# Rotary halves of the queries and keys exchanged by ScalarE copies instead of a product with a constant matrix

## The chip, the cores and the metric

The kernel runs on one core of a Trainium2 chip. The metric is the time of one execution on the device in microseconds (us), as the median over the runs of a kernel. All data are 32-bit floats.

The engines are called as the profile calls them: PE (TensorE, matrix products), PEld (its weight loads), DVE (VectorE), ACT (ScalarE), POOL (GpSimd) and SP (SyncE, which here only issues the weight DMAs). SBUF is the on-chip memory of 128 partitions, PSUM the eight accumulation banks that PE writes.

## The reference, cut to what matters

Two layers of attention plus a mixture of experts on 512 tokens of width 1024, followed by a second block. Only the start of each of the two layers is touched: the query, key and value projections and the rotary embedding of queries and keys.

```python
def rope(t, cos, sin):
    half = t.shape[-1] // 2
    t1, t2 = t[..., :half], t[..., half:]
    return jnp.concatenate([t1 * cos - t2 * sin, t2 * cos + t1 * sin], axis=-1)

for l in range(DEPTH):                       # DEPTH = 2
    proj = x @ w_in[l]                       # (512, 1024) @ (1024, ...)
    q, k, v, cb, cc, cu, qm, gates = jnp.split(proj, IN_SPLITS, axis=-1)
    q = rope(q.reshape(B, S, 16, 64), cos, sin)
    k = rope(k.reshape(B, S, 16, 64), cos, sin)
    ...                                      # attention, convolution, memory attention, merge, experts
```

A head vector has 64 entries; the first 32 and the last 32 are its two halves. Each half is multiplied by the cosine, and the other half, multiplied by the sine (with a minus sign for the first half), is added.

## The kernel before

**Stage.** `qkv` (L736 to L805) is one stage per layer. It makes six chunks n = 0 to 5, each the product of the tokens (`XT`, features in partitions) with a 1024 x 512 slice of `w_in`. Chunks 0 and 1 are the queries, 2 and 3 the keys, 4 and 5 the values. For queries and keys a chunk leaves four tiles c = 0 to 3 of 128 x 512 in `raw` (buffers `B[3]`, `B[4]`), features in partitions, two head vectors of 64 in each tile. The rotated result goes to `out` (`B[0]`, `B[1]`).

**Seven products.** `SevenProducts` (L541 to L723) computes a chunk as a 2 x 2 block product with seven block products instead of eight. The weight sums that this needs are made by POOL (`sum_weights`, L579 to L589: four adds of 128 x 1024 for each chunk, SBUF to SBUF). The token sums are made once in a stage by DVE (L572 to L577). PE runs the seven parts of a chunk (`multiply`, L591 to L664) in the order first, fifth, sixth, third, seventh, second, fourth for n > 0; each part is two halves i = 0, 1 of four 128x256 products, all issued from L600. ACT copies parts out of PSUM as they come (`keep_first`, `keep_fifth`, `keep_sixth`, `last_quarter`; all recorded as L728). DVE adds the rest (`add_sums`: `upper_right` L693, `corner` L699, `upper_left` L705). PE waits for some of it inside the chunk: sixth half i waits for `keep_first` half i (L636), third for `keep_fifth` (L616), seventh for `keep_sixth` (L643), and fourth half i waits for `corner` half i (L622), because it accumulates into the bank that `corner` has read.

**Rotary.** In chunks n = 1 to 4, PE pauses after the first part (`pause`, L650) and runs `rotate(n - 1)` (L759 to L766): for each of the four tiles of the chunk before, one 128x128 by 128x512 product with the constant `rotate`, a signed permutation matrix, into bank 6 or 7. DVE does `turn(n - 1)` (L785 to L797) before the `add_sums` of chunk n: four products tile x cosine (L789), then for each tile bank x sine (L793) and the sum (L796). Each product of `rotate` for c = 2, 3 waits until DVE has read the bank of c - 2 (L764).

**Order.** Every engine runs its own instruction list in the order written; they meet by semaphores. A stage ends in a barrier of all engines. The weight chunks come through a ring of four 2 MB slots; SP issues the load of chunk n + 2 (and its sums get their slot) when the fourth part of chunk n is done (`last_use`, L664). POOL's sums for chunk n + 1 start when that load has landed, which is during chunk n.

**Sine table.** `angle_tables` makes `sin` and `cos` (128 x 512 each) once at the start, `sin` by one ACT instruction (L480). The constants, `rotate` among them, are loaded by one DMA; PE waits for it just before its first `rotate` (L761).

Of the kernel before, what the change touches and what calls it, by code (L numbers as in the profile page):

```python
# [23 lines left out]
ALU = mybir.AluOpType  # L24
ACT = mybir.ActivationFunctionType
AX = mybir.AxisListType.X

P = 128
# [22 lines left out]
TWO_PI_1, TWO_PI_2, TWO_PI_3 = 6.28125, 0.0019340515136718750, 1.2556659146e-06  # L51


CONST_NAMES = ["ident", "ones", "ones_over_d", "head_ones", "rotate", "causal", "earlier",
               "chunk_lower", "chunk_upper", "chunk_upper_incl"]


def constants():
    i = np.arange(P)
    chunk = i // 32  # L60
    same = chunk[:, None] == chunk[None, :]
    rot = np.zeros((P, P), np.float32)
    for m in range(P):
        if m % 64 < 32:
            rot[m + 32, m] = -1.0
        else:
            rot[m - 32, m] = 1.0
    tables = {
        "ident": np.eye(P),
        "ones": np.ones((P, P)),  # L70
        "ones_over_d": np.full((P, P), 1.0 / D),
        "head_ones": (i[:, None] // 64 == i[None, :] // 64),
        "rotate": rot,
        "causal": np.where(i[None, :] <= i[:, None], 0.0, -1e30),
        "earlier": (i[:, None] < i[None, :]),
        "chunk_lower": same & (i[:, None] > i[None, :]),
        "chunk_upper": same & (i[:, None] < i[None, :]),
        "chunk_upper_incl": same & (i[:, None] <= i[None, :]),
    }
    c = np.stack([tables[n] for n in CONST_NAMES], 1).astype(np.float32)  # L80
    t = np.arange(SEQ)
    rows = np.stack([np.broadcast_to(t % 32 != 0, (P, SEQ)), np.broadcast_to(t, (P, SEQ))], 1)
    inv_freq = (10000.0 ** (-np.arange(0, 64, 2) / 64)).astype(np.float32)
    small = np.zeros((P, 64), np.float32)
    small[:, 0] = inv_freq[i % 32]
    small[:, 1:17] = 16 - np.arange(16)
    small[:, 17:21] = 4 - np.arange(4)
    small[:, 24:24 + N_OVER] = np.arange(N_OVER) * P
    small[:, 48:64] = np.arange(E_N) * P
    return c, rows.astype(np.float32), small  # L90


INV_FREQ, EXPERT_KEY, GROUP_KEY = slice(0, 1), slice(1, 17), slice(17, 21)
OVER_START, HOME_SLOT = slice(24, 24 + N_OVER), slice(48, 64)


# [213 lines left out]
class Machine:  # L310
    def __init__(self, nc, ctx, dram):
        self.nc, self.ctx, self.dram = nc, ctx, dram
        sb, sem = self.sb, self.sem
        self.const = sb("const", [P, len(CONST_NAMES), P])
        self.small = sb("small", [P, 64])
# [32 lines left out]
    def sb(self, name, shape, dt=F32):  # L348
        return self.ctx.enter_context(self.nc.sbuf_tensor(name, shape, dt))
# [4 lines left out]
    def c(self, name):  # L354
        return self.const[:, CONST_NAMES.index(name), :]

# [29 lines left out]
    def issue_weights(self, block):  # L386

        @block.sync
        def _(sp):
            static = {n: i for i, n in enumerate(static_names())}  # L390
            while self.issued < len(self.stream):
# [3 lines left out]
                if i == 1:  # L395
                    sp.wait_ge(self.ring_full[0], 16)
                    sp.wait_ge(self.x_loaded, 16)
                    for dst, src in ((self.const[:, :, :], self.dram["consts"]), (self.par[:, :], self.dram["params"]),
                                     (self.rt[:, 3 * P:4 * P], self.dram["consts"][:, CONST_NAMES.index("causal"), :])):
                        sp.dma_start(dst, src).then_inc(self.loaded, 16)  # L400
# [58 lines left out]
def angle_tables(m):  # L459

    ang, k, half = m.T[0], m.T[1], m.T[2]
    with m.stage() as block:
        @block.vector
        def _(dve):
            pos = m.B[4][:, 0, :].bitcast(I32)
            dve.tensor_copy(ang[:, :], pos).then_inc(m.tally("dve_step").up(), 1)
            dve.wait_ge(*m.tally("dve_step").last())
            dve.tensor_scalar(ang[:, :], ang[:, :], m.small[:, INV_FREQ], None, ALU.mult).then_inc(m.tally("dve_step").up(), 1)
            dve.wait_ge(*m.tally("dve_step").last())
            reduce_angle(m, dve, ang, k)  # L470

    with m.stage() as block:
        @block.sync
        def _(sp):
            for dst, src in ((m.memT[:, :, :], m.dram["memT"]), (m.wr[:, :, :], m.dram["w_router"])):
                sp.dma_start(dst, src).then_inc(m.memory_loaded, 16)

        @block.scalar
        def _(act):
            act.activation(m.sin[:, :], ang[:, :], ACT.Sin)  # L480
            act.activation(half[:, :], ang[:, :], ACT.Sin, scale=0.5).then_inc(m.tally("half_sine").up(), 1)

        @block.vector
        def _(dve):
            dve.wait_ge(*m.tally("half_sine").at(1))
            dve.tensor_tensor(half[:, :], half[:, :], half[:, :], ALU.mult).then_inc(m.tally("dve_step").up(), 1)
            dve.wait_ge(*m.tally("dve_step").last())
            dve.tensor_scalar(m.cos[:, :], half[:, :], -2.0, 1.0, ALU.mult, ALU.add)
# [43 lines left out]
def blocks(*tiles):  # L532

    out = []
    for t in tiles:
        v = t.rearrange("p (q a) (b t) -> p q (a b) t", a=2, b=2)
        out += [v[:, i] for i in range(2)]
    return out
# [187 lines left out]
def copy_to(dest):  # L726

    return lambda act, p, h, i, src: act.activation(dest(p, h, i), src, ACT.Copy)  # L728


def within(tile):

    return lambda p, h, i: tile(2 * p + i)[:, HALF * h:HALF * h + HALF]


def qkv(m, l):  # L736

    bk = m.banks
    raw = [m.B[3], m.B[4]]
    out = [m.B[0], m.B[1]]  # L740
    seven = SevenProducts(m, m.XT, blocks(m.B[5][:, 0:4, :], m.B[5][:, 4:8, :]))

    def dest(n):
        if n < 4:
            return within(lambda c: raw[n // 2][:, 4 * (n % 2) + c, :])
        return lambda p, h, i: m.B[2][:, 2 * (2 * h + i) + n - 4, HALF * p:HALF * p + HALF]

    with m.stage() as block:
        for n in range(6):
            seven.chunk(("in", l, n))  # L750
            if 0 < n < 5:
                for c in range(4):
                    bk.plan(("rot", l, n - 1, c), 6 + c % 2)

        @block.tensor
        def _(pe):
            pe.wait_ge(m.x_loaded, 16)

            def rotate(n):  # L759
                if (l, n) == (0, 0):  # L760
                    pe.wait_ge(m.loaded, m.load_n)  # L761
                for c in range(4):
                    seven.finished(pe, n, c // 2, c % 2)
                    pe.wait_ge(*bk.vacant(("rot", l, n, c)))  # L764
                    bank = bk.bank(("rot", l, n, c))
                    pe.matmul(bank[:, :], m.c("rotate"), raw[n // 2][:, 4 * (n % 2) + c, :], start=True, stop=True).then_inc(bk.full_sem(("rot", l, n, c)), 1)  # L766

            for n in range(6):
                seven.multiply(pe, n, tokens_left=n >= 4, pause=(lambda: rotate(n - 1)) if 0 < n < 5 else None)

        @block.scalar
        def _(act):
            for n in range(6):
                for part in (seven.keep_first, seven.keep_fifth, seven.keep_sixth, seven.last_quarter):
                    part(act, n, copy_to(dest(n)))

        @block.gpsimd
        def _(pool):
            for n in range(6):
                seven.sum_weights(pool, n)  # L780

        @block.vector
        def _(dve):

            def turn(n):  # L785
                tile = lambda c: (raw[n // 2][:, 4 * (n % 2) + c, :], out[n // 2][:, 4 * (n % 2) + c, :])
                for c in range(4):
                    seven.finished(dve, n, c // 2, c % 2)
                    dve.tensor_tensor(tile(c)[1], tile(c)[0], m.cos[:, :], ALU.mult).then_inc(m.tally("dve_step").up(), 1)  # L789
                for c in range(4):  # L790
                    dve.wait_ge(*bk.made(("rot", l, n, c)))
                    tmp = m.T[c % 2]
                    dve.tensor_tensor(tmp[:, :], bk.bank(("rot", l, n, c))[:, :], m.sin[:, :], ALU.mult).then_inc(bk.free_sem(("rot", l, n, c)), 1)  # L793
                    dve.wait_ge(*bk.read_done(("rot", l, n, c)))
                    dve.wait_ge(*m.tally("dve_step").last())
                    dve.tensor_tensor(tile(c)[1], tile(c)[1], tmp[:, :], ALU.add).then_inc(m.tally("dve_step").up(), 1)  # L796
                    dve.wait_ge(*m.tally("dve_step").last())  # L797

            dve.wait_ge(m.x_loaded, 16)
            seven.sum_tokens(dve)  # L800
            for n in range(6):
                if 0 < n < 5:
                    turn(n - 1)
                seven.add_sums(dve, n, dest(n))
        m.issue_weights(block)  # L805


# [2386 lines left out]
```

## Time and profile before

| | us |
|---|---|
| median of 3 runs (3727.48 to 3737.3) | 3736.56 |
| profiled execution, its own time | 3742.89 |
| span of that execution | 3741.2 |
| PE busy | 3309.7 (88%) |
| PEld busy | 2272.8 (61%) |
| DVE busy | 1497.7 (40%) |
| POOL busy | 769.6 (21%) |
| ACT busy | 715.3 (19%) |

The mean granted clock of TensorE over the span is 0.928 of full speed. In the profile a row `L600 PE MATMUL bank<-B,ring` is the group of PE products issued by line 600 that write a PSUM bank from buffer B and the weight ring; a bracket at the end of a row is the idle time of the engine before it and who ended it. A 32-bit product of one PE instruction in the code shows as two records. "2.99 PE x6" is six records merged over 2.99 us. The four busy shares of an average over the whole span say little about one stage, so the prediction reads the stage itself.

### The profile page before, as it was taken

The numbers are of one execution on the slowest core, as the hardware profiler recorded it, in microseconds if no ns is written. First come the engines' busy times: TensorE is split into PE (matmuls) and PEld (weight loads), VectorE is DVE, ScalarE is ACT, GpSimd is POOL, SyncE is SP. The second block draws the span as 40 slices with busy tenths as digits, with TensorE's granted clock in tenths as the row PEclk, the third lists the DMA queues.
The fourth block names the chain that finished last, engine by engine and source line by source line (L and its number), as shares of the span: only waits on it lengthen the run. The fifth ranks groups of instructions, "written<-read, shape, count | busy, mean of one in ns | idle before, by whom it ended". The sixth has DMA issues, their size and how long they took to land. (4 is left out here: it accounts for less than half of the span.)

```text
span 3741.2 us, 37361 instructions
## 1 busy us (share of the span) xinstructions
PE 3309.7 (88%) x14316; PEld 2272.8 (61%) x14316; DVE 1497.7 (40%) x2645; ACT 715.3 (19%) x1630; POOL 769.6 (21%) x490
## 2 busy tenths in 40 slices
PE   6989999959998598999998699947789899699996
PEld 5857767744444486776666344426567667488842
DVE  4364712331111545576644111134567522455502
ACT  1152211021111114323221111112222111111100
POOL 3314112300000340311002100003344322243200
PEclk9989999969999798999998899978889889899998
DMA  3141222227887111032232588832101122112210
GB/s 140 68 192 50 108 79 79 90 101 285 320 326 270 68 68 46 28 131 79 113 118 90 212 326 325 319 143 93 65 24 46 47 90 90 45 68 90 112 68 23
DMA packets 49365, 471.22 MB, mean 126 GB/s; under 512 B 5600, under 2 KB 5984, under 8 KB 25376
## 3 DMA queue, kind: packets, MB, share of 16 engines
q1 hardware_dynamic: 26784, 378.77, 27.6%
q0 software_dynamic: 20816, 76.03, 5.1%
q10 hardware_dynamic: 1584, 13.93, 0.9%
q8 instruction: 123, 2.02, 0.2%
q14 instruction: 58, 0.48, 0.0%
HBM read 507.76 MB, written 63.70 MB: 153 GB/s over the span
## 5 line engine op out<-in xcount | busy, mean ns | idle before, releaser
L600 PE MATMUL bank<-B,ring 128*128 128x256 f32 x4336 | 957.2, 381 | 38.1 <-PEq L1985 21.3
L600 PEld LDWEIGHTS bank<-B,ring 128*128 128x128 f32 x4336 | 828.5, 191 | 165.0 <-issue 49.4
L1788 PE MATMUL bank<-ring,B 128*128 128x512 f32 x1024 | 451.4, 599 | 1.8 <-issue 1.5
L584 POOL TENSOR_TENSOR ring<-ring 128x1024 f32<-128x1024 f32 x52 | 134.6, 2589 | 1258.7 <-DMA ring<-in_w_static 341.2
L728 ACT ACTIVATE B<-bank 128x256 f32<-128x256 f32 x356 | 135.8, 383 | 1117.6 <-PE bank L600 1093.9
L600 PE MATMUL bank<-XT,ring 128*128 128x256 f32 x1344 | 307.9, 383 | 45.0 <-PEq L812 28.9
L1788 PEld LDWEIGHTS bank<-ring,B 128*128 128x128 f32 x1024 | 193.7, 192 | 237.2 <-issue 235.0
L600 PEld LDWEIGHTS bank<-XT,ring 128*128 128x128 f32 x1344 | 258.2, 193 | 86.5 <-issue 51.3
L509 PE MATMUL bank<-B,ring 128*128 128x512 f32 x704 | 307.8, 596 | 2.0 <-issue 2.0
L509 PEld LDWEIGHTS bank<-B,ring 128*128 128x128 f32 x704 | 134.7, 191 | 164.6 <-issue 163.8
L1856 DVE TENSOR_TENSOR B<-B,bank 128x512 f32<-128x512 f32 x46 | 31.6, 687 | 492.7 <-PE bank L1788 480.7
L1807 PE MATMUL bank<-ring,B 128*128 128x512 f32 x512 | 226.3, 595 | 1.5 <-ACT B L1841 1.5
L1807 PEld LDWEIGHTS bank<-ring,B 128*128 128x128 f32 x512 | 95.0, 190 | 110.0 <-issue 110.0
L2976 PE MATMUL bank<-B,ring 128*128 128x512 f32 x352 | 153.8, 600 | 7.3 <-PEq L2888 7.3
L693 DVE TENSOR_TENSOR B<-bank,B 128x256 f32<-128x256 f32 x96 | 40.4, 424 | 280.7 <-PE bank L600 280.1
L588 POOL TENSOR_TENSOR ring<-ring 128x1024 f32<-128x1024 f32 x52 | 136.5, 2626 | 4.1
L586 POOL TENSOR_TENSOR ring<-ring 128x1024 f32<-128x1024 f32 x52 | 136.5, 2625 | 4.1
L1867 DVE COPY B<-bank 128x512 f32<-128x512 f32 x92 | 62.3, 690 | 184.6 <-PE bank L1807 182.0
L589 POOL TENSOR_TENSOR ring<-ring 128x1024 f32<-128x1024 f32 x52 | 134.1, 2578 | 0.0
L2976 PEld LDWEIGHTS bank<-B,ring 128*128 128x128 f32 x352 | 67.7, 193 | 93.0 <-issue 93.0
L699 DVE TENSOR_TENSOR B<-bank,B 128x256 f32<-128x256 f32 x98 | 41.6, 424 | 156.8 <-PE bank L600 156.8
L1832 ACT ACTIVATE B<-bank 128x512 f32<-128x512 f32 x92 | 50.3, 600 | 263.7 <-PE bank L1757 174.2
(439 smaller groups left out, 3928.2 us busy)
## 6 DMA issues: line engine op xcount, KB each, us to landing
ring<-in_w_expert SPq DMA_DIRECT2D x96, 2048.0 KB, 9.0
ring<-in_w_static SPq DMA_DIRECT2D x79, 2048.0 KB, 8.0
B<-in_w_expert SPq DMA_DIRECT2D x42, 2048.0 KB
slots_y<-B POOLq DMA_DIRECT2D x53, 512.0 KB, 27.1
B<-slots_x POOLq DMA_DIRECT2D x46, 512.0 KB
slots_x<-B POOLq DMA_DIRECT2D x23, 512.0 KB, 16.0
ring<-s_tables SPq DMA_DIRECT2D x4, 2048.0 KB, 7.8
s_tables<-tmp POOLq DMA_DIRECT2D x8, 512.0 KB, 3.8
```

The lines of the kernel that those rows point to most:

```text
L509: ins = pe.matmul(bank[:, :], w(k, col), rhs(k), start=k == 0, stop=k == kts - 1)
L584: pool.tensor_tensor(s(0), w(1, 0), w(1, 1), ALU.add).then_inc(made.up(), 1)
L586: pool.tensor_tensor(s(1), s(0), w(0, 0), ALU.subtract).then_inc(made.up(), 1)
L588: pool.tensor_tensor(s(3), w(0, 1), s(1), ALU.subtract).then_inc(made.up(), 1)
L589: pool.tensor_tensor(s(2), w(0, 0), w(1, 0), ALU.subtract).then_inc(made.up(), 1)
L600: ins = pe.matmul(out, left, right, start=start and k == 0, stop=k == 3, skip_group_check=not start)
L728: return lambda act, p, h, i, src: act.activation(dest(p, h, i), src, ACT.Copy)
L1788: ins = pe.matmul(bank[:, :], xbT[q % 2][:, k, :], slot[:, k, :], start=k == 0, stop=k == KT - 1)
L1807: ins = pe.matmul(bank[:, :], hidT[q % 2][:, k, :], slot[:, k, cols], start=k == 0, stop=k == 3)
L1832: act.activation(xbT[q % 2][:, 4 * i:4 * i + 4, :], bank[:, :].rearrange("p (a b) -> p a b", a=4), ACT.Copy).then_inc(bk.free_sem(("xbT", ...
L1867: dve.tensor_copy(y[o % 2][:, i, :], bank[:, :]).then_inc(bk.free_sem(("y", l, o, i)), 1)
L2976: ins = pe.matmul(bank[:, :], slot(k % 4, c), hidden_tile(m, k), start=k == 0, stop=k == FF_T - 1)
```

## The change

The constant `rotate` is dropped. `sin` gets its sign in the table: the ACT instruction that makes it takes a per-partition scale, -1 in the first 32 partitions of each 64 and +1 in the others (sin(-a) = -sin(a)). PE has no `rotate` and no pause. ACT copies the halves of each tile of `raw` crosswise into `out` (`exchange`: four copies of 32 partitions x 512 for each tile), one tile behind each of its existing parts of the chunk. DVE then multiplies `out` by the signed sine into a scratch tile, writes tile x cosine over `out`, and adds the scratch; it does tiles 0 and 1 before `add_sums` of the chunk and tiles 2 and 3 behind it. Banks 6 and 7 are no longer used in this stage.

```diff
-            act.activation(m.sin[:, :], ang[:, :], ACT.Sin)
+            act.activation(m.sin[:, :], ang[:, :], ACT.Sin, scale=m.small[:, HALF_SIGN])
...
@@ qkv, tensor engine
-            def rotate(n):
-                if (l, n) == (0, 0):
-                    pe.wait_ge(m.loaded, m.load_n)
-                for c in range(4):
-                    seven.finished(pe, n, c // 2, c % 2)
-                    pe.wait_ge(*bk.vacant(("rot", l, n, c)))
-                    bank = bk.bank(("rot", l, n, c))
-                    pe.matmul(bank[:, :], m.c("rotate"), raw[n // 2][:, 4 * (n % 2) + c, :], start=True, stop=True).then_inc(bk.full_sem(("rot", l, n, c)), 1)
             for n in range(6):
-                seven.multiply(pe, n, tokens_left=n >= 4, pause=(lambda: rotate(n - 1)) if 0 < n < 5 else None)
+                seven.multiply(pe, n, tokens_left=n >= 4)
+            if l == 0:
+                pe.wait_ge(m.loaded, m.load_n)
...
@@ qkv, scalar engine
+            def exchange(n, c):
+                seven.finished(act, n, c // 2, c % 2)
+                src, dst = raw[n // 2][:, 4 * (n % 2) + c, :], out[n // 2][:, 4 * (n % 2) + c, :]
+                for to, fro in ((0, 32), (32, 0), (64, 96), (96, 64)):
+                    ins = act.activation(dst[to:to + 32, :], src[fro:fro + 32, :], ACT.Copy)
+                ins.then_inc(m.tally("exchanged").up(), 1)
             for n in range(6):
-                for part in (seven.keep_first, seven.keep_fifth, seven.keep_sixth, seven.last_quarter):
+                for c, part in enumerate((seven.keep_first, seven.keep_fifth, seven.keep_sixth, seven.last_quarter)):
+                    if 0 < n < 5 and c == 3:
+                        exchange(n - 1, 3)
                     part(act, n, copy_to(dest(n)))
+                    if 0 < n < 5 and c < 3:
+                        exchange(n - 1, c)
...
@@ qkv, vector engine
-            def turn(n):
+            def turn(n, pair):
                 tile = lambda c: (raw[n // 2][:, 4 * (n % 2) + c, :], out[n // 2][:, 4 * (n % 2) + c, :])
-                for c in range(4):
-                    seven.finished(dve, n, c // 2, c % 2)
-                    dve.tensor_tensor(tile(c)[1], tile(c)[0], m.cos[:, :], ALU.mult)...
-                for c in range(4):
-                    ...
+                step = m.tally("dve_step")
+                for c in pair:
+                    dve.wait_ge(*m.tally("exchanged").at(4 * n + c + 1))
+                    dve.tensor_tensor(m.T[c % 2], tile(c)[1], m.sin[:, :], ALU.mult).then_inc(step.up(), 1)
+                dve.wait_ge(*step.last())
+                for c in pair:
+                    dve.tensor_tensor(tile(c)[1], tile(c)[0], m.cos[:, :], ALU.mult).then_inc(step.up(), 1)
+                dve.wait_ge(*step.last())
+                for c in pair:
+                    dve.tensor_tensor(tile(c)[1], tile(c)[1], m.T[c % 2], ALU.add).then_inc(step.up(), 1)
+                dve.wait_ge(*step.last())
...
                 if 0 < n < 5:
-                    turn(n - 1)
+                    turn(n - 1, (0, 1))
                 seven.add_sums(dve, n, dest(n))
+                if 0 < n < 5:
+                    turn(n - 1, (2, 3))
```

## Rows read from the trace of the kernel before

**Rows 1.** Stretches: length, busy us (instructions) by engine, granted clock, DMA share, GB/s.
```profile
55.72:84.17 28.45, 28.08 (x121) 22.64 (x120) 11.97 (x18) 3.07 (x8) 10.20 (x4) 1.00 0.20 75
169.54:194.00 24.46, 24.34 (x113) 21.09 (x111) 2.55 (x6) 3.16 (x9) 0.00 (x0) 1.00 0.23 86
1327.07:1355.52 28.45, 28.08 (x121) 22.63 (x120) 11.97 (x18) 3.07 (x8) 9.96 (x4) 1.00 0.20 74
```

**Rows 2.** Timeline of PE: start us, length us, records; first layer, then second.
```profile
55.72 3.62 PE L600 MATMUL bank<-XT,ring 128*128 128x256 f32 x16
59.17 2.99 PE L766 MATMUL bank<-B,const 128*128 128x512 f32 x6
62.52 1.10 PE L766 MATMUL bank<-B,const 128*128 128x512 f32 x2 [0.35 <-DVE tmp L793]
63.45 7.07 PE L600 MATMUL bank<-B,ring 128*128 128x256 f32 x32
...
148.82 7.07 PE L600 MATMUL bank<-ring,B 128*128 128x256 f32 x32
172.99 7.07 PE L600 MATMUL bank<-ring,B 128*128 128x256 f32 x32
...
1298.61 1.67 PE L600 MATMUL bank<-XT,ring 128*128 128x256 f32 x7
```

**Rows 3.** Instructions of line 766: durations in ns (minimum, median, maximum).
```profile
L766 PE MATMUL bank<-B,const x64: 592/592/668, 59.2 to 1391.3; 128*128 128x512 f32 x64
```

**Rows 4.** Timeline of ACT in chunk 1 of the first layer.
```profile
57.65 0.38 ACT L728 ACTIVATE B<-bank 128x256 f32<-128x256 f32 x1 [1.34 <-PE bank L600]
59.37 0.38 ACT L728 ACTIVATE B<-bank 128x256 f32<-128x256 f32 x1 [1.34 <-PE bank L600]
65.38 0.38 ACT L728 ACTIVATE B<-bank 128x256 f32<-128x256 f32 x1 [5.62 <-PE bank L600]
```

**Rows 5.** Groups of ACT instructions: busy us, mean ns; first a timeline row.
```profile
294.76 4.26 ACT L1074 ACTIVATE B<-B 128x512 f32<-128x512 f32 x8
...
L2468 ACT ACTIVATE B<-B 64x512 f32<-64x512 f32 x1 | 0.6, 630 | 0.0
L977 ACT ACT_TABLE_LOAD x3 | 3.8, 1283 | 3.5 <-PE bank L864 3.5
```

**Rows 6.** Timeline of POOL in the qkv stages.
```profile
35.59 3.21 POOL L588 TENSOR_TENSOR ring<-ring 128x1024 f32<-128x1024 f32 x1
63.91 2.85 POOL L584 TENSOR_TENSOR ring<-ring 128x1024 f32<-128x1024 f32 x1 [12.33 <-DMA ring<-in_w_static]
120.63 2.35 POOL L584 TENSOR_TENSOR ring<-ring 128x1024 f32<-128x1024 f32 x1 [17.92 <-DMA ring<-in_w_static]
123.06 2.68 POOL L586 TENSOR_TENSOR ring<-ring 128x1024 f32<-128x1024 f32 x1
125.82 2.68 POOL L588 TENSOR_TENSOR ring<-ring 128x1024 f32<-128x1024 f32 x1
128.46 2.35 POOL L589 TENSOR_TENSOR ring<-ring 128x1024 f32<-128x1024 f32 x1
1307.29 2.37 POOL L584 TENSOR_TENSOR ring<-ring 128x1024 f32<-128x1024 f32 x1 [12.40 <-DMA ring<-in_w_static]
```

**Rows 7.** Timeline of DVE in the qkv stage of the first layer.
```profile
30.05 3.25 DVE L574 TENSOR_TENSOR B<-XT,B 128x1024 f32<-128x1024 f32 x1
33.23 3.37 DVE L575 TENSOR_TENSOR B<-XT 128x1024 f32<-128x1024 f32 x1
61.69 0.69 DVE L793 TENSOR_TENSOR tmp<-bank,rotary 128x512 f32<-128x512 f32 x1
75.81 0.42 DVE L699 TENSOR_TENSOR B<-bank,B 128x256 f32<-128x256 f32 x1 [1.30 <-PE bank L600]
81.33 1.28 DVE L789 TENSOR_TENSOR B<-B,rotary 128x512 f32<-128x512 f32 x2
120.77 2.77 DVE L796 TENSOR_TENSOR B<-B,tmp 128x512 f32<-128x512 f32 x1
124.29 2.00 DVE L796 TENSOR_TENSOR B<-B,tmp 128x512 f32<-128x512 f32 x1
...
39.81 0.74 DVE L705 TENSOR_TENSOR B<-bank,B 128x256 f32<-128x256 f32 x2
```

**Rows 8.** Stretches of the attention stages of both layers, columns as in rows 1.
```profile
194.00:290.00 96.00, 78.42 (x368) 50.62 (x368) 68.29 (x256) 56.78 (x201) 16.99 (x31) 0.79 0.48 187
1437.00:1534.00 97.00, 79.65 (x368) 50.62 (x368) 68.11 (x256) 57.86 (x202) 0.00 (x0) 0.77 0.06 22
```

More of the change, by code:

```diff
@@ L51 @@
 TWO_PI_1, TWO_PI_2, TWO_PI_3 = 6.28125, 0.0019340515136718750, 1.2556659146e-06
-CONST_NAMES = ["ident", "ones", "ones_over_d", "head_ones", "rotate", "causal", "earlier",
+CONST_NAMES = ["ident", "ones", "ones_over_d", "head_ones", "causal", "earlier",
                "chunk_lower", "chunk_upper", "chunk_upper_incl"]
@@ L61, in constants @@
     same = chunk[:, None] == chunk[None, :]
[L62 to L67, printed above, removed]
     tables = {
@@ L72, in constants @@
         "head_ones": (i[:, None] // 64 == i[None, :] // 64),
-        "rotate": rot,
         "causal": np.where(i[None, :] <= i[:, None], 0.0, -1e30),
@@ L89, in constants @@
     small[:, 48:64] = np.arange(E_N) * P
+    small[:, 21] = np.where(i % 64 < 32, -1.0, 1.0)
     return c, rows.astype(np.float32), small
-INV_FREQ, EXPERT_KEY, GROUP_KEY = slice(0, 1), slice(1, 17), slice(17, 21)
+INV_FREQ, EXPERT_KEY, GROUP_KEY, HALF_SIGN = slice(0, 1), slice(1, 17), slice(17, 21), slice(21, 22)
 OVER_START, HOME_SLOT = slice(24, 24 + N_OVER), slice(48, 64)
@@ L750, in qkv @@
             seven.chunk(("in", l, n))
-            if 0 < n < 5:
-                for c in range(4):
-                    bk.plan(("rot", l, n - 1, c), 6 + c % 2)
         @block.tensor
@@ L783, in _ @@
         def _(dve):
-            def turn(n):
+            def turn(n, pair):
                 tile = lambda c: (raw[n // 2][:, 4 * (n % 2) + c, :], out[n // 2][:, 4 * (n % 2) + c, :])
-                for c in range(4):
-                    seven.finished(dve, n, c // 2, c % 2)
[L789 to L797, printed above, removed]
+                step = m.tally("dve_step")
[9 more added lines that the diff above has]
+                dve.wait_ge(*step.last())
             dve.wait_ge(m.x_loaded, 16)
```

## The prediction

> **What bounds the kernel now.** The busy shares of the whole span name PE (88%), but the change touches only two stages, so I read those. First the table of stretches: chunks 1 to 4 of `qkv` take 28.45 us each with PE busy for 28.08, chunk 5, which has no pause, 24.46 with 24.34, both at granted clock 1.00, the full 2.4 GHz [rows 1]. DVE is busy for 12 us of such a chunk, ACT for 3, POOL for 10. So PE bounds the stage. Then PE's timeline, to see what it does with the difference: between the end of the first part (59.17) and the start of the fifth (63.45) stand eight records of the product with `rotate`, and one idle gap of 0.35 that DVE's reading of a bank ended [rows 2]. Last the timelines of ACT, DVE and POOL in one chunk, for what the new work meets there. The chain of waits that the page prints covers only the end of the program, so I don't use it.
>
> **What is removed.** One pause is 63.45 - 59.17 = 4.28 us. The distance from fifth part to fifth part confirms it: 172.99 - 148.82 = 24.17 without a pause between them, and 28.45 - 24.17 = 4.28 [rows 1, 2]. There are four in each layer and the layers have the same pace [rows 1]: 8 x 4.28 = 34.2 us. The 64 records of 0.592 us [rows 3] overlap, and their sum of 37.9 would count too much. PE has no other work to wait for in that place, so all of it leaves the path if PE is not held up elsewhere.
>
> **Where PE could be held up: a chunk in its own time.** Let t = 0 be the start of a chunk. Seven parts at 24.17 / 7 = 3.45 us start at: first 0, fifth 3.45, sixth 6.91, third 10.36, seventh 13.81, second 17.27, fourth 20.72; each half is 1.73 later. ACT gets a half 1.93 after its part's start (57.65 - 55.72) and takes 0.38 [rows 2, 4].
>
> **ACT.** It gains 16 copies in each of these chunks, in four groups. No row has ACT write other partitions than it reads, nor 32 of them. The nearest are 128x512 SBUF to SBUF, eight in 4.26 us, so 0.62 for one and 0.52 from one to the next; 64x512 takes 0.63, so fewer partitions save nothing [rows 5]. I take these: a group is 3 x 0.52 + 0.62 = 2.18. Ends of the range: 0.38, the row of half as many elements [rows 4], and 1.28, the table load, ACT's longest instruction there [rows 5]. With 2.18:
> `keep_first` ends at 3.65 + 0.38 = 4.03; exchange of tile 0 ends 6.21; `keep_fifth` 6.59 and (its second half is ready at 7.10) 7.48; exchange 1 ends 9.66; `keep_sixth` 10.04 and 10.93; exchanges 2 and 3 end at 15.3; `last_quarter` is ready only at 22.65. PE wants `keep_first` by 6.91 and 8.64, `keep_fifth` by 10.36 and 12.09, `keep_sixth` by 13.81 and 15.54. Every one is more than 3 us early. At 0.38 a copy exchange 1 would end at about 8.7, and what follows would be the same. ACT costs nothing; what hides it is that ACT is idle for over 25 of 28.45 us [rows 1].
>
> **DVE and POOL.** This is where I expect a cost. DVE's instruction count in a chunk stays (12 for the rotation, 6 sums), but bank x sine becomes `out` x sine. Before, it read PSUM. The rows show what that is worth: while POOL adds, DVE instructions that read a bank keep their 0.42 or 0.69, and those with two SBUF inputs don't: L796 takes 0.69 alone, but issued at 120.77, just behind POOL's add of 120.63, it took 2.77 and ended at 123.54, 0.56 after POOL's end at 122.98 [rows 6, 7]. POOL's add was undisturbed (2.35), and the next one, met by the DVE one, took 2.68 [rows 6]. They take turns even where DVE issues without a wait: L575 at 33.23 follows L574 at once and still took 3.37, with POOL's 3.21 beside it [rows 6, 7].
>
> In the Trainium skill, the page "SBUF — State Buffer", section "SBUF: two separate sides", calls this an exclusive lock on a shared port pair that the loser waits out, against the notion that both share bandwidth. At half speed each, the five instructions from 9.7 on would take 6.9 us and end by 16.6, and the time would be that of rival A below; by the lock it is my forecast. The trace agrees with the lock, by the 2.77 beside an undisturbed 2.35.
>
> When does POOL run? Its adds begin when the next weights have landed: in the third chunk with a pause that is at t = 8.0 (120.63 less its start, 55.72 + 2 x 28.45), in the second layer's first at 8.7 (1307.29 - 1298.61) [rows 2, 6]; these are the earliest and the latest of eight, and I take 8.33. The load is issued at the chunk's start as before, so this doesn't move. Four adds then. The old `turn` was nearly through by then; the new one begins at 6.2 and is caught:
> tile 0 x sine 6.2 to 6.9, free. Tile 1 x sine is issued at 9.7, in POOL's first add (8.33 to 10.68), ends 11.24. From there they alternate; POOL's adds end 2.76 apart (0.08 + 2.68), the last 2.64 after: 10.68, 13.44, 16.20, 18.84. Tile 0 x cosine ends 14.0, tile 1 x cosine 16.8, the first sum 19.4, the second, POOL being done, 0.59 later at 19.99 (two in a row take 1.28). Then `add_sums`: from 20.03 two `upper_right`, 0.32 apart as the two in 0.74, then `corner` half 0, issued at 20.67, done at 21.09. PE resumes 0.14 after the DVE result that it waits for (62.52 - 61.69 - 0.69) [rows 2, 7]: 21.23. It wanted to start the fourth part at 20.72. So the wait that ends last is now `corner` for PE's fourth part, 0.51 us in each of the eight chunks: 4.1 us in all (0.2 each with POOL at 8.0, 0.9 with 8.7). `corner` half 1 comes 0.32 later and is wanted 1.73 later: free.
>
> Then two `upper_left` and the pair of tiles 2 and 3: six instructions at 0.59 to 0.69 from t = 22.0 to about 26, that is until 1.5 us into the next chunk; DVE is next wanted at 6.2 there. Their exchanges were done at 15.3. The last such pair lies under chunk 5. Banks read by `upper_right` and `upper_left` are wanted by PE in the next chunk only.
>
> **The rest.** The sine's scale in a column: the same one instruction. A 64 KB smaller constant load, and PE's wait for it at the end of the stage instead of at 59: it was no wait even there [rows 2]. Weight loads and POOL: a chunk must be landed and summed in 24.17 us; sums are done at t = 18.8 of the chunk before. Chunk 5 shows the faster pace. The attention stage follows a barrier and moves as a whole; its granted clock was 0.79 and 0.77 in the two layers, with about 1 us between their lengths [rows 8], which is the size of chance there.
>
> **Sum.** Against the profiled execution: 3742.89 - 34.2 + 4.1 = 3712.8 (span 3741.2, so 1.7 around it, unchanged). Its time is 6.3 above the median of the runs; by the median the forecast is 3736.56 - 30.1 = 3706.5.
>
> **Rivals.**
> A, no stall: DVE gets between POOL's adds faster than one for one, or they start later or earlier against it, and `corner` is in time. What is missing is only 0.51, which speaks for it; L575 speaks against it. Time 3736.56 - 34.2 = 3702.3.
> B, copies across partitions cost more. At 1.28 each: exchange 0 ends 9.15, exchange 1 15.03, `keep_sixth` 15.41, so the seventh part starts at 15.55 instead of 13.81, and `corner` is in time for the fourth that this delays: 1.74 x 8 = 13.9, 3716.3. Of the same sign, and counted here, is one more DVE instruction behind POOL's adds (+0.7 each, 3712). For it: no row shows such a copy. Against: ACT's rows of 512 elements take 0.62 and 0.63 [rows 5].
> C, slower than before: ACT becomes the bound of the stage. In a chunk it has 16 copies and eight of 0.38, 3.07 in all; that passes 24.17 at 1.32 us a copy and the old 28.45 at 1.59, which is where the change turns to a loss. At 2.0 us a chunk takes 35.1, and the time is 3736.6 + 8 x 6.6 = 3790. It would need a price over two and a half times that of the rows taken.
> D, no change: copies between 1.45 and 1.6 us, or stalls near 3 us in each chunk. POOL has only four adds to stand in the way, so DVE alone can't make it.
>
> **Chances.** Forecast 0.55, A 0.2, B (with one more blocked instruction) 0.15, D 0.06, C 0.04. What a measurement of this kernel tells from no change is about 0.3%, 11 us. Forecast, A and B are all faster by more: 0.90; within 0.06; slower 0.04. The range: A's 3702 less 8 for the spread of the runs (3727 to 3737 before), up to B's 3716 and a little of that spread: 3694 to 3718. With C and D outside, over 8 in 10 are inside.
>
> **What would show it.** Chunks 1 to 4 at 24.7 us instead of 28.45; an idle gap of PE of 0.2 to 0.9 us before the fourth part, ended by DVE's `corner`; four DVE instructions of 1.5 to 2.8 us in each chunk while POOL adds; ACT copies of 0.62 in groups of 2.2; granted clock 1.00 throughout. I am wrong if PE waits for an ACT copy, if the stretches outside `qkv` change by more than 5 us, or if no gap stands before the fourth part.

## The result, and the profile after

The changed kernel takes 3706.7 us (median of 5 runs, 3700.7 to 3709.0), the kernel before 3737.3 beside it (5 runs, 3727.5 to 3740.7). The ratio is 0.9914 with a 95% interval of 0.9901 to 0.9926: faster by 28 to 37 us. The forecast was 3706.5; the profiled execution took 3700.7 (span 3698.9, before 3741.2).

The stretches of five of the eight changed chunks (four in each layer), with the columns of [rows 1]:

```profile
55.07:79.72 24.65, 24.41 (x113) 21.20 (x112) 15.07 (x17) 13.10 (x24) 10.47 (x4) 1.00 0.24 86
79.72:104.22 24.50, 24.41 (x113) 21.20 (x112) 16.11 (x19) 13.11 (x24) 10.47 (x4) 1.00 0.23 86
104.22:129.65 25.43, 24.41 (x113) 21.20 (x112) 17.04 (x19) 13.11 (x24) 10.46 (x4) 1.00 0.23 83
129.65:155.49 25.84, 24.42 (x114) 21.20 (x113) 17.45 (x19) 13.11 (x24) 10.49 (x4) 1.00 0.23 82
...
1329.51:1353.97 24.46, 24.41 (x113) 21.20 (x112) 16.07 (x19) 13.11 (x24) 10.50 (x4) 1.00 0.24 87
```

A chunk takes 24.46 to 25.84 us instead of 28.45. The three that are not shown take 24.61, 24.51 and 24.69. All eight come to 198.7 us against 227.6: 28.9 less. PE's busy time is the same in each (24.41), so what varies is idle time. ACT went from 3.1 to 13.1 us busy, DVE from 12.0 to between 15 and 17.5 with hardly more instructions: they became longer. PE's timeline shows where the idle time lies (first chunk, then the end of the fourth; here and below only the rows that bear on the point are shown):

```profile
55.07 3.62 PE L594 MATMUL bank<-XT,ring 128*128 128x256 f32 x16
58.53 7.07 PE L594 MATMUL bank<-B,ring 128*128 128x256 f32 x32
72.34 3.62 PE L594 MATMUL bank<-XT,ring 128*128 128x256 f32 x16
76.19 3.69 PE L594 MATMUL bank<-B,ring 128*128 128x256 f32 x16 [0.23 <-DVE B L693]
...
146.92 3.62 PE L594 MATMUL bank<-ring,XT 128*128 128x256 f32 x16
151.96 3.69 PE L594 MATMUL bank<-ring,B 128*128 128x256 f32 x16 [1.42 <-DVE B L693]
```

The fifth part follows the first at once (58.53 - 55.07 = 3.46). The only gap is before the fourth part, ended by `corner` (now L693): 76.19 comes 3.85 after 72.34 where 3.45 is due, so 0.40; in the fourth chunk 5.04 - 3.45 = 1.59. The brackets give 0.17 less, because the shown length of a part (3.62) is longer than the distance to the next (3.45); the distances between starts are used here for the size of a gap.

DVE and POOL in the first chunk, each a timeline:

```profile
65.16 0.88 DVE L786 TENSOR_TENSOR tmp<-B,rotary 128x512 f32<-128x512 f32 x1 [2.76 <-ACT B L762]
66.08 5.48 DVE L789 TENSOR_TENSOR B<-B,rotary 128x512 f32<-128x512 f32 x2
71.60 3.33 DVE L792 TENSOR_TENSOR B<-B,tmp 128x512 f32<-128x512 f32 x2
74.96 0.76 DVE L687 TENSOR_TENSOR B<-bank,B 128x256 f32<-128x256 f32 x2
75.63 0.75 DVE L693 TENSOR_TENSOR B<-bank,B 128x256 f32<-128x256 f32 x2
```

```profile
63.15 2.35 POOL L578 TENSOR_TENSOR ring<-ring 128x1024 f32<-128x1024 f32 x1 [11.73 <-DMA ring<-in_w_static]
65.58 2.68 POOL L580 TENSOR_TENSOR ring<-ring 128x1024 f32<-128x1024 f32 x1
68.33 2.68 POOL L582 TENSOR_TENSOR ring<-ring 128x1024 f32<-128x1024 f32 x1
70.98 2.79 POOL L583 TENSOR_TENSOR ring<-ring 128x1024 f32<-128x1024 f32 x1
```

The lock that the Trainium skill's page "SBUF — State Buffer" (section "SBUF: two separate sides") describes is seen here at work: two products with the cosine take 5.48 us instead of the 1.28 of two such instructions alone [rows 7], and POOL's second to fourth adds 2.68 to 2.79 instead of the 2.35 of its first. POOL's last add ends at 73.77, DVE's last sum at 74.93. `corner` half 0 is the first of the two instructions of L693: it starts at 75.63 and, at 0.42, ends at 76.05. PE starts at 76.19.

The copies of ACT, all 128 of them, with durations in ns (minimum, median, maximum), and a timeline row of one group:

```profile
L762 ACT ACTIVATE B<-B x128: 625/628/631, 59.1 to 1369.4; 32x512 f32<-32x512 f32 x128
...
59.13 2.54 ACT L762 ACTIVATE B<-B 32x512 f32<-32x512 f32 x4
```

A second profile of the same kernel, taken for the comparison at the end of the experiments, has the same picture: the eight chunks come to 197.9 us, and the gaps are 0.22 to 1.17 us, 3.9 in all.

### The profile page after: what moved, and what is told of

Read it like the earlier page. It is cut to its first block and busy times, and to the rows that moved or that the text cites. A ratio compares the mean times of both kernels' runs of the same rounds, so it can differ in the third digit from the quotient of the medians.

```text
span 3698.9 us, 37279 instructions
## 1 busy us (share of the span) xinstructions
PE 3269.8 (88%) x14252; PEld 2254.9 (61%) x14252; DVE 1537.2 (42%) x2645; ACT 795.7 (22%) x1758; POOL 773.5 (21%) x490
## 3 DMA queue, kind: packets, MB, share of 16 engines
q1 hardware_dynamic: 26784, 378.70, 28.1%
## 5 line engine op out<-in xcount | busy, mean ns | idle before, releaser
L687 DVE TENSOR_TENSOR B<-bank,B 128x256 f32<-128x256 f32 x96 | 39.6, 423 | 223.3 <-PE bank L594 222.5
L1881 POOL DMA_DIRECT2D B<-slots_x x32 | 17.4, 545 | 386.4 <-PE bank L1755 192.9
```

## The experiments

Theory L: the pause was PE's own time and its loss is the gain; what is given back is DVE's waiting behind POOL's adds, which makes `corner` late. Its rivals are named with each run. A time after the word "median" has its ratio to the kernel before, run on the same chip.

**Rotation behind the sums.** All of DVE's rotation moves to where POOL is idle.

```diff
-                if 0 < n < 5:
-                    turn(n - 1, (0, 1))
                 seven.add_sums(dve, n, dest(n))
                 if 0 < n < 5:
+                    turn(n - 1, (0, 1))
                     turn(n - 1, (2, 3))
```

> DVE does the rotation of all four tiles behind `add_sums` of the chunk instead of half of it ahead. Theory L (DVE waits out POOL's adds, and `corner` is late by that): the rotation then runs from about t = 22 to t = 6 of the next chunk, when POOL is idle; no gap before the fourth part, chunks 1 to 4 at 24.17 us instead of 24.5 to 25.8, 5.3 us less over the eight, so about 3701. Theory M (the gap comes from ACT's slow exchanges, which reach DVE late): the same here, since `corner` no longer stands behind them. Theory N (the gap is PE's own or comes with the pace of the weights): chunks stay at 24.5 to 25.8.

Median 3701.8, ratio 0.9916 (0.9902 to 0.9930). The three pairs of instructions shown each take 1.28 or 1.29 again, behind `corner`, and PE's second and fourth parts of the first chunk stand 3.45 apart, with no bracket:

```profile
72.97 3.62 PE L594 MATMUL bank<-XT,ring 128*128 128x256 f32 x16
76.42 3.62 PE L594 MATMUL bank<-B,ring 128*128 128x256 f32 x16
...
77.03 1.28 DVE L786 TENSOR_TENSOR tmp<-B,rotary 128x512 f32<-128x512 f32 x2
78.35 1.29 DVE L789 TENSOR_TENSOR B<-B,rotary 128x512 f32<-128x512 f32 x2
```

All eight chunks are 24.17 or 24.18 us. Theory N (the gap is PE's own) falls; L and M (the gap comes from exchanges that end late) stand.

**POOL held.** Only POOL's adds move; ACT and DVE keep their order.

```diff
             for n in range(6):
+                if n > 1:
+                    pool.wait_ge(*m.tally("dve_step").at(12 * (n - 2) + 6))
                 seven.sum_weights(pool, n)
```

> Only POOL's adds for the next chunk are held until DVE has rotated tiles 0 and 1; ACT and DVE keep their order. Theory L: the five DVE instructions take 0.69 each again, `add_sums` is ahead of its products, no gap before the fourth part, chunks at 24.17, about 3701. POOL starts at t = 13.5 and is through by 23.2, before the sums are wanted at 27.6. Theory M: the exchanges end as before, so the gap stays at 0.2 to 1.6 us and the chunks at 24.5 to 25.8.

Median 3700.0, ratio 0.9909 (0.9895 to 0.9924). The exchanges are as late as in the changed kernel (DVE starts tile 1 at 65.98 - 55.89 = 10.09), but DVE's instructions are short and POOL's add is back at 2.36:

```profile
65.98 0.69 DVE L788 TENSOR_TENSOR tmp<-B,rotary 128x512 f32<-128x512 f32 x1 [2.76 <-ACT B L762]
66.71 1.29 DVE L791 TENSOR_TENSOR B<-B,rotary 128x512 f32<-128x512 f32 x2
68.03 1.29 DVE L794 TENSOR_TENSOR B<-B,tmp 128x512 f32<-128x512 f32 x2
...
77.63 2.45 DVE L788 TENSOR_TENSOR tmp<-B,rotary 128x512 f32<-128x512 f32 x2
...
73.16 3.62 PE L594 MATMUL bank<-XT,ring 128*128 128x256 f32 x16
76.61 3.62 PE L594 MATMUL bank<-B,ring 128*128 128x256 f32 x16
...
69.41 2.36 POOL L578 TENSOR_TENSOR ring<-ring 128x1024 f32<-128x1024 f32 x1 [18.02 <-DVE B L794]
```

The fourth part follows the second at 3.45 (73.16 to 76.61), and chunks are 24.17 (55.89 to 80.06). Theory M falls: the lateness of the exchanges alone makes no gap. DVE and POOL still meet: POOL's last add now catches the first product of tiles 2 and 3 (2.45 us for two, at 77.63), but that is behind `corner`, and PE waits for nothing there.

**POOL released at the worst moment.** The same wait, but for exchange 1 (`m.tally("exchanged").at(4 * (n - 2) + 2)`).

> POOL's adds for the next chunk are held until ACT has made exchange 1, the moment at which DVE issues tile 1 x sine, instead of until DVE is through. In the eight chunks of the changed kernel the gap before the fourth part was POOL's start less 7.67 us. Theory L: with a start at about t = 10.15 all of tile 1 x sine, both cosines and the first sum are caught, the gap is 10.15 - 7.67 = 2.5 us in every chunk, chunks of 26.7 us, 8 x 2.5 = 20 us over the kernel with POOL held to the end of the rotation (3700): about 3720. If a wait on POOL, or its later adds, as such had removed the gap there: none here either, 3700.

Median 3724.4, ratio 0.9962 (0.9950 to 0.9975). All four instructions behind tile 1 x sine are caught, and every chunk has the gap, 2.36 to 2.39 us (the first: 77.77 - 71.93 - 3.45 = 2.39):

```profile
64.81 2.86 POOL L578 TENSOR_TENSOR ring<-ring 128x1024 f32<-128x1024 f32 x1 [13.46 <-ACT B L762]
...
65.50 5.49 DVE L791 TENSOR_TENSOR B<-B,rotary 128x512 f32<-128x512 f32 x2
71.02 5.48 DVE L794 TENSOR_TENSOR B<-B,tmp 128x512 f32<-128x512 f32 x2
...
77.77 3.69 PE L594 MATMUL bank<-B,ring 128*128 128x256 f32 x16 [2.22 <-DVE B L693]
...
131.02 5.38 PE L594 MATMUL bank<-B,ring 128*128 128x256 f32 x16 [2.21 <-DVE B L693]
```

Against the kernel with POOL held the median is 24 us higher and the mean of the runs 21. Six of the eight chunks are 26.6 us, and eight of that length would give 20. In the profiled execution two of the eight fourth parts also ran slower behind their gaps, 5.38 (shown) and 5.30 instead of 3.69, at a granted clock of 0.67 in the stretch of the first, which adds 3.3. So the same wait of POOL either removes the gap or makes it largest, by its moment alone. Together with the changed kernel's own eight chunks this is one line within 0.1 us: the gap is POOL's start less 7.65 to 7.68 in the eight, and less 7.75 here (t counts from the chunk's start):

| chunk | POOL starts at t | gap before the fourth part |
|---|---|---|
| layer 1, chunks 1 to 4 | 8.08, 7.93, 8.86, 9.25 | 0.40, 0.25, 1.18, 1.59 |
| layer 2, chunks 1 to 4 | 8.04, 7.93, 7.87, 8.10 | 0.36, 0.26, 0.22, 0.44 |
| released with exchange 1, first chunk | 10.14 (64.81 - 54.67) | 2.39 |

In the second profile of the changed kernel seven of the eight gaps are POOL's start less 7.64 to 7.68. The eighth has the earliest start of all, 7.75, and a gap of 0.22 instead of 0.08: tile 1 x sine was issued 0.02 us before POOL's first add ended and took its 0.69, and POOL's second add took 2.81 instead of 2.68.

**Exchanges left out.** DVE reads `raw` for the product with the sine and doesn't wait for ACT. The kernel leaves out that each half takes the other's entries, so its rotation is wrong; only its times are of use.

```diff
-                    dve.wait_ge(*m.tally("exchanged").at(4 * n + c + 1))
-                    dve.tensor_tensor(m.T[c % 2], tile(c)[1], m.sin[:, :], ALU.mult)...
+                    seven.finished(dve, n, c // 2, c % 2)
+                    dve.tensor_tensor(m.T[c % 2], tile(c)[0], m.sin[:, :], ALU.mult)...
```

> ACT's exchanges are left out, and DVE multiplies the tile itself by the sine (the other half of each head is not used; the result is a wrong rotation). DVE's order stays. Theory L: tiles 0 and 1 need not wait for ACT, so their six instructions follow the pair before at once and end by about t = 6, ahead of POOL's start at 8: no gap, chunks of 24.17 us, about 3701. The exchanges thus cost nothing as work of ACT, only by moving DVE's rotation into POOL's window. If DVE's rotation as such (its six instructions ahead of the sums) makes `corner` late: gaps as in the changed kernel, 3706.

Median 3705.3 (4 runs, 3697.1 to 3705.8), ratio 0.9917 (0.9901 to 0.9934). The profile is as expected: chunks of 24.17, no gap before the fourth part (99.33 - 95.88 = 3.45), and in the second chunk, shown here, the pair of tiles 0 and 1 over at 83.69, well before POOL's first add:

```profile
95.88 3.62 PE L594 MATMUL bank<-XT,ring 128*128 128x256 f32 x16
99.33 3.62 PE L594 MATMUL bank<-B,ring 128*128 128x256 f32 x16
...
82.40 1.29 DVE L788 TENSOR_TENSOR B<-B,tmp 128x512 f32<-128x512 f32 x2
...
86.51 2.35 POOL L578 TENSOR_TENSOR ring<-ring 128x1024 f32<-128x1024 f32 x1 [14.74 <-DMA ring<-in_w_static]
```

By its median alone this run would fit the other expectation (3706) as well: it is 4 above what the chunks give. Its runs spread by 9 us, and four don't settle it, so the reading rests on the trace, where no chunk has a gap.

**Exchanges made twice, and three times.** Each group of four copies is repeated, with a wait of ACT on itself between.

```diff
-                for to, fro in ((0, 32), (32, 0), (64, 96), (96, 64)):
-                    ins = act.activation(dst[to:to + 32, :], src[fro:fro + 32, :], ACT.Copy)
+                for again in range(2):          # 3 in the second kernel
+                    for to, fro in ((0, 32), (32, 0), (64, 96), (96, 64)):
+                        ins = act.activation(dst[to:to + 32, :], src[fro:fro + 32, :], ACT.Copy)
+                    ...
```

> Every exchange is made twice (32 copies of ACT in a chunk, one wait of ACT on itself in each exchange). If ACT is hidden until its chain through a chunk is longer than PE's: a group takes 5.15 us, exchange 0 ends 9.2, exchange 1 15.2, the seventh part starts near 15.8 instead of 13.81, exchange 3 ends near 26.4, so `last_quarter` frees PE's bank near 26.8 and a chunk takes about 27 us: 8 x (27.0 - 24.8) = 17 us over the changed kernel, about 3724, still under the 3737 of before. If ACT's work is hidden by its idle time alone (23.7 of 24.2 us busy): no change, 3707.

> Every exchange is made three times (48 copies of ACT in a chunk), to see whether ACT can turn the gain into a loss. A group of 12 takes 7.75 us. ACT then has 4 x 7.75 + 3.07 = 34.1 us in a chunk, more than PE's 24.17 and than the 28.45 of before: chunks of about 34 to 37 us, 8 x (34 to 37 - 28.45) = 44 to 68 us over the kernel before, 3780 to 3805. If ACT can't bound the stage: no more than the 3719 of the doubled copies.

Twice: median 3719.3, ratio 0.9957 (0.9941 to 0.9973), 5 us below the expectation. Three times: 3817.4, ratio 1.0222 (1.0202 to 1.0242), 12 above the expected range. PE's timelines, twice and then three times:

```profile
70.03 3.69 PE L594 MATMUL bank<-B,ring 128*128 128x256 f32 x16 [1.62 <-POOL ring L582]
81.04 3.69 PE L594 MATMUL bank<-XT,ring 128*128 128x256 f32 x16 [0.41 <-ACT B L722]
```

```profile
67.60 3.69 PE L594 MATMUL bank<-XT,ring 128*128 128x256 f32 x16 [1.79 <-ACT B L722]
76.00 6.25 PE L594 MATMUL bank<-B,ring 128*128 128x256 f32 x16 [4.71 <-ACT B L722]
92.12 6.72 PE L594 MATMUL bank<-XT,ring 128*128 128x256 f32 x16 [2.96 <-ACT B L722]
...
76.00:82.09 6.09, 6.09 (x17) 4.95 (x17) 3.94 (x8) 5.92 (x11) 0.00 (x0) 0.57 0.00 0
```

Twice: the seventh part starts 1.78 us late, by the starts (the third part starts at 64.80: 70.03 - 64.80 - 3.45; bracket 1.62), for want of `keep_sixth`, and the next first part 0.57 late (bracket 0.41) for want of `last_quarter`; chunks of 26.6 to 26.7 (the first bracket names POOL, but in the later chunks the same gap is put down to ACT, whose copy ended then). The fourth part has hardly a gap of its own any more (0.03 at most). Three times: gaps of 1.8, 4.7 and 3.0 in the first chunk by the brackets (the last is 2.5 to 4.2 in others), and behind the long ones PE is slower: the parts take 6.3 and 6.7 us instead of 3.7, at a granted clock of 0.57 of full speed in the stretch of the one at 76.00 (last row, columns of [rows 1]). The chunks of the first layer are 36.8 to 39.9 us. The expectation had only ACT's time in it, and its upper end was passed by 1.5 us a chunk; the slower parts, 5.6 us for the two shown, are the likely cause, though no run takes them away.

**The pause kept.** The changed kernel with four products of PE put back into each pause (unit matrix, results unused).

```diff
+            def filler(n):
+                ...
+                for c in range(4):
+                    seven.finished(pe, n, c // 2, c % 2)
+                    pe.matmul(bk.ps[6 + c % 2][:, :], m.c("ident"), raw[n // 2][:, 4 * (n % 2) + c, :], start=True, stop=True)
-                seven.multiply(pe, n, tokens_left=n >= 4)
+                seven.multiply(pe, n, tokens_left=n >= 4, pause=(lambda: filler(n - 1)) if 0 < n < 5 else None)
```

> The changed kernel with PE's four products of 128x512 put back in each pause (stationary the unit matrix, results unused). If the 4.28 us of the pause are PE's own time: 3.93 us return in each chunk (4.28 less the gap of 0.35 that DVE caused), and `corner` is in time again, as the fourth part is later by more than the gap: chunks at 28.1, 8 x (28.1 - 24.84) = 26 us more than the changed kernel, about 3733. If the gain came from DVE or ACT: well under 20 us more.

Median 3732.4, ratio 0.9990 (0.9979 to 1.0001). Almost all of the gain is gone, with ACT's copies and DVE's new order still in place. What is left by the time, 0.0010 or 4 us, is not clear of noise (by the chunks it is 8 x 0.85 = 6.8):

```profile
57.97 3.60 PE L755 MATMUL bank<-B,const 128*128 128x512 f32 x8
61.40 7.07 PE L594 MATMUL bank<-B,ring 128*128 128x256 f32 x32
78.67 3.62 PE L594 MATMUL bank<-B,ring 128*128 128x256 f32 x16
```

The products take 61.40 - 57.97 = 3.43 us and the fourth part (78.67) has no gap; chunks are 27.60 (54.52 to 82.12), not the 28.1 expected. These products do not wait for DVE to free their bank, as `rotate` did. So of the 4.28 of the old pause, 3.43 were products and 0.85 went with that wait; the bracket in [rows 2] showed 0.35 of it, and the expectation took it for the whole.

**Forms of the copy.** One form in each chunk, four in the last. The kernel leaves out the crossing in most of them; only its times are of use.

> The copies of ACT in other forms, one kind for each chunk (the queries and keys are then rotated with the wrong halves, in all but the first chunk). In the changed kernel four crossed copies of 32 partitions start 0.64 us apart, each 0.63 long, while eight 128x512 instructions of ACT started 0.52 apart. Chunk 1: crossed, as before, 0.64. Chunk 2: four copies of 32 partitions, each onto its own partitions. Chunk 3: three copies of all 128 partitions. Chunk 4, tile 0: two crossed copies of 64; tile 1: two copies of partitions 0 to 31 onto themselves; tile 2: two of 32 to 63 onto 0 to 31; tile 3: two of 64 to 127 onto themselves. If crossing prevents the overlap: 0.64 in chunk 1 and tiles 0 and 2, 0.52 elsewhere. If a change of the first partition from one instruction to the next prevents it: 0.64 in chunks 1 and 2 and tile 0, 0.52 in chunk 3 and tiles 1, 2 and 3. If fewer than 128 partitions do: 0.52 in chunk 3 alone. If it is copies from SBUF as such: 0.64 everywhere.

A single run (3701.5 us); the timeline of ACT is what it was for. In order: crossed 32, straight 32 (both four in a group), whole tiles, crossed 64, then twice partitions 0 to 31 onto themselves with a whole tile behind, and twice 32 to 63 onto 0 to 31 with a whole tile behind:

```profile
59.57 2.54 ACT L773 ACTIVATE B<-B 32x512 f32<-32x512 f32 x4
84.03 2.54 ACT L773 ACTIVATE B<-B 32x512 f32<-32x512 f32 x4
109.22 1.15 ACT L773 ACTIVATE tmp<-B 128x512 f32<-128x512 f32 x2
133.66 1.27 ACT L773 ACTIVATE B<-B 64x512 f32<-64x512 f32 x2
136.98 1.13 ACT L773 ACTIVATE tmp<-B 32x512 f32<-32x512 f32 x2
138.02 0.61 ACT L773 ACTIVATE B<-B 128x512 f32<-128x512 f32 x1
140.56 1.15 ACT L773 ACTIVATE tmp<-B 32x512 f32<-32x512 f32 x2
141.73 0.63 ACT L773 ACTIVATE B<-B 128x512 f32<-128x512 f32 x1
```

Two that keep their first partitions take 1.13 to 1.15, so the second starts 0.5 us after the first; this holds for the pair that crosses (140.56) too, and for the last form, two copies of partitions 64 to 127 onto themselves, not shown (1.15). Where the first partition, read or written, changes from one to the next, crossed or not, they don't overlap: 2.54 for four, 1.27 for two, and the whole tile at 141.73 starts 1.17 after its pair began, the one at 138.02, which keeps first partition 0, only 1.04. Neither crossing nor the number of partitions matters in these forms.

**The two best beside each other.** Changed kernel and rotation behind the sums, again, on one chip.

> The changed kernel itself, beside the one with the rotation behind the sums on the same chip. Its chunks 1 to 4 at 24.5 to 25.8 us with a gap before each fourth part, 4 to 6 us slower than the other: about 3706.

> The same kernel as e1_turn_behind_sums, beside the changed one on the same chip: chunks at 24.17 us, about 3701. If the two are within 2 us of each other, the gap before the fourth part is made up elsewhere.

Medians 3706.7, ratio 0.9923 (0.9908 to 0.9939), and 3700.4, ratio 0.9905 (0.9890 to 0.9920). Beside each other (six runs of each) the means differ by 5.5 us, 95% interval 1 to 10. Over all runs of each (11 and 12, on more than one chip) the means are 3706.6 and 3702.6, a difference of 3.9 us with an interval of 1.0 to 6.9; the chunks give 5.3. So the version with the rotation behind the sums is faster than both kernels; the one with POOL held is the same as it by its times and chunks. Nothing is left in these chunks beside PE's seven parts.

## Why the prediction was right

**The pause** was right: 28.45 to 24.17 where nothing stalls. The kept pause shows that the gain comes from PE's own list and not from the engines around it.

**The gap before the fourth part** was right in place, cause and size. It was put at 0.51 in each chunk, at POOL's start less 7.82; measured are 0.22 to 1.59, mean 0.59, at POOL's start less 7.67 in all eight. The spread of the starts was too narrow (8.0 to 8.7 taken; 7.9 to 9.25), and their mean a little too late (8.33 taken, 8.26). The sum of the gaps is 4.7 us instead of 4.1 (3.9 in the second profile), and 0.08 in each is lost again as the part behind a gap takes 3.53 instead of 3.45. Rival A, no gap, is refuted by the changed kernel's trace, and the runs that take the meeting away have no gap.

**Luck** is in the last digits. The chunks alone give 28.9 us, the forecast had 30.1, and the medians are 30.6 apart; that forecast and median agree within 0.2 us is chance, with runs that spread by 8 us and more.

**The term that was mis-sized** is ACT's group of four copies: 2.54 us, not 2.18, because the copies don't overlap. Exchange 1 ends at t = 10.1, not 9.66. It cost nothing, because that is still inside POOL's first add (until 10.4); and ACT had over 3 us in hand everywhere. The 0.15 us between 7.82 and 7.67 are mostly POOL's last add, which ended 2.76 after the one before, not 2.64. How long DVE's first caught instruction waits has no part in it: tile 1 x sine took 0.88, 0.74, 1.67 and 2.06 us in the four chunks, but ended 0.55 us after POOL's first add each time.

**Rivals B and C** did not occur, but their mechanism is real: at double the work, which is 1.29 us for a copy, ACT holds the seventh part back by 1.78 where 1.74 was worked out for 1.28; at three times, 1.9 us for a copy, it turns the gain into a loss of 80 us. The turning point, put at 1.59 us for a copy, lies between the two and was not measured. Beyond it the prediction's line is too flat: at 1.9 us it gives a loss of some 45 us, likely because the slower products behind long gaps are not in it.

**What I named as proof against me** happened in one point: the stretches outside the eight chunks differ by more than 5 us between the two profiles (42.3 less span, 28.9 of it in the chunks, so 13.4 outside). From the start of the second attention stage to the end, the kernel before took 3741.2 - 1437.7 = 2303.5 and the changed one 3698.9 - 1403.9 = 2295.0. In the second profile of the same changed kernel it took 3706.0 - 1404.6 = 2301.4, and 5.5 are left outside the chunks. So most of it belongs to that one execution, not to the change; the criterion was too narrow for single executions, whose times spread by 11 us (changed, 11 runs) to 19 us (before, 17 runs) within one kernel. The difference of the medians, 30.6, is within 2 us of the chunks'.

## What to carry to other kernels

On the engine that bounds a stage, even small products in a pause are paid in full (3.43 us of every 27.60 here), while an engine that was idle for nine tenths of the chunk could take four instructions for one, as long as its chain through the step stays under the other's. When a step moves from PSUM to SBUF on VectorE, look at what GpSimd does in that window: two engines that never wait for each other by semaphore can still take turns, and which of them sits where is a free choice of order. Then place the work in time, not only on an engine: the same six VectorE instructions cost 0.7 us a chunk ahead of the sums and nothing behind them.

## What the runs showed of the hardware that was not expected

Neighbouring ScalarE copies overlapped by about 0.1 us only where both read from the same first partition and both wrote to the same: 2.54 us for four copies at changing first partitions, 1.13 to 1.15 for two at the same. A copy of 512 columns that writes other partitions than it reads took the same 0.63 us, and 32 partitions took what 128 did (0.61 to 0.63).

PE ran at full clock up to each of the following gaps (sizes by the brackets). One of 2.2 us before a part was followed in two of eight cases by a slower part (5.38 and 5.30 us instead of 3.7, granted clock 0.67 and 0.68 of full speed), those of 2.5 to 4.7 us by a slower one each time (5.1 to 6.8 us, granted clock 0.57 in the stretch shown), those of 1.6 and 1.8 us never.

When VectorE instructions with two SBUF inputs meet GpSimd adds, the two take turns one instruction at a time (2.74 us for each VectorE one, 2.68 to 2.79 for each add), so how late VectorE ends here is set by when GpSimd starts, not by when VectorE is ready.
